# Expert lists of a mixture-of-experts block, computed at the width that each rank can hold

## The reference, cut to what matters

```python
def moe(h, router_w, router_bias, w1, w3, w2):
    ...
    _, top_idx = lax.top_k(jnp.where(in_group, sel, -jnp.inf), TOP_K)     # TOP_K = 2
    ...
    gate = jnp.sum(jax.nn.one_hot(top_idx, N_EXPERTS, dtype=f) * wts[..., None], axis=1).astype(t.dtype)
    out = jnp.zeros_like(t)
    for e in range(N_EXPERTS):
        hid = jax.nn.silu(t @ w1[e]) * (t @ w3[e])
        out = out + gate[:, e:e + 1] * (hid @ w2[e])
    return out.reshape(shp)
```

## Time and profile before

| | |
|---|---|
| median of 3 runs | 1711.62 us |
| the profiled execution's own time | 1710.11 us |
| its span | 1708.4 us |
| TensorE busy | 1548.5 us, 91% |
| VectorE busy | 1027.1 us, 60% |
| ScalarE busy | 777.4 us, 46% |
| listed steps in the trace, w3 of step 1 to w2 of step 12 | about 681 us to 929 us |
| mean granted clock of TensorE | 0.943 |

### The profile page before, as it was taken

One profiled execution on the slowest core, in us unless ns is written; L12 is line 12 of the kernel. 1 busy time (PEld: TensorE's weight loads), 2 busy tenths in 40 slices (PEclk: granted clock), 3 DMA queues, 4 the chain that ended last, 5 costly groups with the idle time before them and its releaser, 6 DMA issues.

```text
span 1708.4 us, 23313 instructions
## 1 busy us (share of the span) xinstructions
PE 1548.5 (91%) x9498; PEld 1297.2 (76%) x9498; DVE 1027.1 (60%) x1288; ACT 777.4 (46%) x937; POOL 231.2 (14%) x303
## 2 busy tenths in 40 slices
PE   4899989797668788999999989999999999999997
PEld 2678776575558667888887767779999777799996
DVE  1557446747555666777775766565444655655445
ACT  4524314551332344666665325535444556444444
POOL 0013361231241012000001350010000000000000
PEclk9899999897679888999999999989999999999999
DMA  9757620010334524898987644325544544345441
GB/s 348 276 213 271 163 50 1 7 25 5 88 97 156 205 100 173 321 325 325 324 317 263 214 148 148 112 79 196 190 175 178 196 148 148 122 163 188 178 179 72
DMA packets 152530, 294.14 MB, mean 172 GB/s; under 512 B 33538, under 2 KB 36745, under 8 KB 152424
## 3 DMA queue, kind: packets, MB, share of 16 engines
q1 hardware_dynamic: 136024, 270.50, 44.7%
q0 software_dynamic: 6464, 18.61, 3.4%
q10 hardware_dynamic: 9936, 3.54, 0.8%
HBM read 283.16 MB, written 9.47 MB: 171 GB/s over the span
## 4 chain that ended last, share of the span: by engine, by line
PE 75%; DVE 8%; issue 5%; ACT 4%; DMA 2%; DVEq 2%; SPq 1%; ACTq 1%; POOL 1%; POOLq 0%
PE psum L214 20%; PE psum L216 20%; PE psum L215 20%; PE psum L2490 3%; DMA modw<-in_mod_w_dram 1%; DVE w_low L2385 1%; PE psum L3491 1%; DMA raw<-in_w_out_dram 1%; PE psum L3515 1%; PE psum L748 1%; DVE w_low L202 1%; PE psum L765 1%; ACT w_high L179 1%; PE psum L1537 1%; DVE outer L1170 1%
## 5 line engine op out<-in xcount | busy, mean ns | idle before, releaser
L184 DVE TENSOR_TENSOR w_low<-raw,w_high 128x4096 fp32r<-128x4096 f32 (+1 forms) x60 | 265.7, 4429 | 253.4 <-ACT w_high L179 253.0
L179 ACT ACTIVATE w_high<-raw 128x4096 fp32r<-128x4096 f32 (+1 forms) x62 | 223.7, 3611 | 136.2 <-DMA raw<-in_w_up_dram 85.5
L2385 DVE TENSOR_TENSOR w_low<-raw,w_high 128x2048 fp32r<-128x2048 f32 x90 | 202.8, 2295 | 43.9 <-ACT w_high L2377 43.6
L2377 ACT ACTIVATE w_high<-raw 128x2048 fp32r<-128x2048 f32 x90 | 165.7, 1908 | 10.2 <-DMA raw<-in_moe_w_dram 10.1
L216 PE MATMUL psum<-actA_high,w_low 128*128 128x256 f32 x512 | 144.9, 283 | 0.0
L215 PE MATMUL psum<-actA_low,w_high 128*128 128x256 f32 x512 | 144.9, 283 | 0.0
L214 PE MATMUL psum<-actA_high,w_high 128*128 128x256 f32 x512 | 144.8, 283 | 0.0
L214 PE MATMUL psum<-w_high,act_high 128*128 128x512 f32 x320 | 127.8, 399 | 15.3 <-DVE act_low L1980 9.0
L215 PE MATMUL psum<-w_low,act_high 128*128 128x512 f32 x320 | 126.3, 395 | 0.0
L216 PE MATMUL psum<-w_high,act_low 128*128 128x512 f32 x320 | 126.1, 394 | 0.0
L214 PE MATMUL psum<-w_high,ff_high 128*128 128x512 f32 x256 | 100.0, 391 | 0.0
(11 more groups left out here) (570 smaller groups left out, 3482.0 us busy)
## 6 DMA issues: line engine op xcount, KB each, us to landing
raw<-in_moe_w_dram SPq DMA_DIRECT2D x90, 1024.0 KB, 6.5
raw<-in_w_in_dram SPq DMA_DIRECT2D x20, 2048.0 KB, 8.6
raw<-in_w_up_dram SPq DMA_DIRECT2D x16, 2048.0 KB, 8.0
raw<-in_w_down_dram SPq DMA_DIRECT2D x16, 2048.0 KB, 7.6
modw<-in_mod_w_dram SPq DMA_DIRECT2D x12, 2048.0 KB, 13.1
raw<-in_w_out_dram SPq DMA_DIRECT2D x6, 2048.0 KB, 8.5
raw<-in_w_gate_dram SPq DMA_DIRECT2D x4, 2048.0 KB, 7.8
raw<-in_moe_w_dram SPq DMA_DIRECT2D x3, 2048.0 KB, 8.3
```

The costliest lines, as they stand in the source:

```text
L179: act.activation(WH[n % NSLOT][:, 0:elems], RAW[n % NSLOT][:, 0:elems], ACT.Copy).then_inc(s_wh, 1)
L184: dve.tensor_tensor(WL[n % NSLOT][:, 0:elems], RAW[n % NSLOT][:, 0:elems], WH[n % NSLOT][:, 0:elems].bitcast(F32), ALU.subtract).then_inc( ...
L2377: act.activation(WH[n % NSLOT][:, ps], RAW[n % NSLOT][:, ps], ACT.Copy).then_inc(s_wh if h else X["fwh"], 1)
L2385: dve.tensor_tensor(WL[n % NSLOT][:, ps], RAW[n % NSLOT][:, ps], WH[n % NSLOT][:, ps].bitcast(F32), ALU.subtract).then_inc(s_wl if h else ...
```

## The change

Each listed step is computed on `slots_of(i)` slots, which is now rounded up to an even number (128, 102, 86, 74, 64, 56, 52, 46, 42, 40, 36, 34): the selection matrix, the moving operand of the gather, the copies into `gact`, the stationary operand of w1, w3 and w2, the partitions of silu, product and `ybuf`, and the width of the split of the hidden list. The number of instructions and their order stay as they are on every engine. There is one gather of 32 matmuls for each listed step, as before. The dense steps keep their shapes.

```diff
+    def slots_at(j):
+        return min(P, (2 * T // (j + 1) + 1) // 2 * 2)
...
     def slots_of(i):
-        return min(P, TOPK * T // (place(i) + 1))
+        return slots_at(place(i))
+
+    def rows_in(i):
+        return slots_of(i) if listed(i) else P
...
         for t in range(NT):
-            ins = pool.tensor_scalar(pickd[i % 2][:, t, :], slot1[:, :], slotk[:, t, j:j + 1], None, ALU.is_equal)
+            n = slots_of(i)
+            ins = pool.tensor_scalar(pickd[i % 2][:, t, 0:n], slot1[:, 0:n], slotk[:, t, j:j + 1], None, ALU.is_equal)
...
                     for t in range(NT):
-                        ins = pe.matmul(psum[:, gather_banks(i)[b], at:at + P], ht[:, t, P * k:P * (k + 1)],
-                                        pickd[i % 2][:, t, :], start=(t == 0), stop=(t == NT - 1))
+                        ins = pe.matmul(psum[:, gather_banks(i)[b], at:at + n], ht[:, t, P * k:P * (k + 1)],
+                                        pickd[i % 2][:, t, 0:n], start=(t == 0), stop=(t == NT - 1))
...
     def gathered(i, b):
-        return gact[i % 2][:, 2 * b:2 * b + 2, :, :].rearrange("p k w n -> p (k w n)")
+        return gact[i % 2][:, 2 * b:2 * b + 2, :, :].rearrange("p k w n -> p (k w) n")[:, :, 0:slots_of(i)]
+
+    def gather_out(i, b):
+        return psum[:, gather_banks(i)[b], :].rearrange("p (q n) -> p q n", n=P)[:, :, 0:slots_of(i)]
...
         if listed(i):
-            return gact[i % 2][:, k, 0, :], gact[i % 2][:, k, 1, :]
+            return gact[i % 2][:, k, 0, 0:slots_of(i)], gact[i % 2][:, k, 1, 0:slots_of(i)]
...
-                ins = three_pass(pe, psum[:, bank + t, :], aH, aL, wh[:, k, :], wl[:, k, :], k == 0, k == KT - 1)
+                ins = three_pass(pe, psum[0:rows_in(i), bank + t, :], aH, aL, wh[:, k, :], wl[:, k, :], k == 0,
+                                 k == KT - 1)
...
-            ins = pe.transpose(psum[:, 2 + t, P * c:P * (c + 1)], hidt[:, t, P * c:P * (c + 1)], ident[:, :])
+            m = rows_in(i)
+            ins = pe.transpose(psum[:, 2 + t, P * c:P * c + m], hidt[0:m, t, P * c:P * (c + 1)], ident[0:m, 0:m])
...
-                ts = slice(P * t, P * (t + 1))
+                ts = slice(P * t, P * t + rows_in(i))
...
-                    ins = three_pass(pe, psum[:, 4 + 2 * t + half, :], hidH[:, k, ts], hidL[:, k, ts], wh[:, k, hs],
+                    ins = three_pass(pe, psum[0:rows_in(i), 4 + 2 * t + half, :], hidH[:, k, ts], hidL[:, k, ts], wh[:, k, hs],
...
-            ins = act.activation(hidH[:, :, P * t:P * (t + 1)], bank3(2 + t), ACT.Copy)
+            m = rows_in(i)
+            ins = act.activation(hidH[:, :, P * t:P * t + m], bank3(2 + t)[:, :, 0:m], ACT.Copy)
...
-            ins = dve.tensor_tensor(hidL[:, :, ts], bank3(2 + t), hidH[:, :, ts].bitcast(F32), ALU.subtract)
+            ins = dve.tensor_tensor(hidL[:, :, ts], bank3(2 + t)[:, :, 0:rows_in(i)], hidH[:, :, ts].bitcast(F32), ALU.subtract)
```

More of the change, by code:

```diff
@@ L1851, in two_block_kernel @@
     posv = lr2.take("posv", [P, NT, E])
-    ROWS = 1 + sum(min(P, 2 * T // (j + 1)) for j in range(3, E - 1))
+    def slots_at(j):
+        return min(P, (2 * T // (j + 1) + 1) // 2 * 2)
+    ROWS = 1 + sum(slots_at(j) for j in range(3, E - 1))
     yrows = nc.dram_tensor("yrows", (ROWS, D), F32, kind="Internal").ap()
@@ L2489, in gather_tensor @@
                     for t in range(NT):
-                        ins = pe.matmul(psum[:, gather_banks(i)[b], at:at + P], ht[:, t, P * k:P * (k + 1)],
-                                        pickd[i % 2][:, t, :], start=(t == 0), stop=(t == NT - 1))
+                        ins = pe.matmul(psum[:, gather_banks(i)[b], at:at + n], ht[:, t, P * k:P * (k + 1)],
+                                        pickd[i % 2][:, t, 0:n], start=(t == 0), stop=(t == NT - 1))
             ins.then_inc(X["gat"], 1)
     def gathered(i, b):
-        return gact[i % 2][:, 2 * b:2 * b + 2, :, :].rearrange("p k w n -> p (k w n)")
+        return gact[i % 2][:, 2 * b:2 * b + 2, :, :].rearrange("p k w n -> p (k w) n")[:, :, 0:slots_of(i)]
+    def gather_out(i, b):
+        return psum[:, gather_banks(i)[b], :].rearrange("p (q n) -> p q n", n=P)[:, :, 0:slots_of(i)]
     def gather_scalar(act, i, b):
         act.wait_ge(X["gat"], since("gat", 4 * (i - 1) + b + 1))
-        act.activation(gathered(i, b), psum[:, gather_banks(i)[b], :], ACT.Copy).then_inc(X["gaA"], 1)
+        act.activation(gathered(i, b), gather_out(i, b), ACT.Copy).then_inc(X["gaA"], 1)
     def gather_vector(dve, i, b):
         dve.wait_ge(X["gat"], since("gat", 4 * (i - 1) + b + 1))
-        dve.tensor_copy(gathered(i, b), psum[:, gather_banks(i)[b], :]).then_inc(X["gaV"], 1)
+        dve.tensor_copy(gathered(i, b), gather_out(i, b)).then_inc(X["gaV"], 1)
     def rows_of(i, k, t):
         if listed(i):
-            return gact[i % 2][:, k, 0, :], gact[i % 2][:, k, 1, :]
+            return gact[i % 2][:, k, 0, 0:slots_of(i)], gact[i % 2][:, k, 1, 0:slots_of(i)]
         ts = slice(P * t, P * (t + 1))
@@ L2643, in silu_scalar @@
             act.wait_ge(M["hid"], i)
-        n = tiles_of(i)
-        act.activation(sgt[:, 0:n, :], psum[:, 0:n, :], ACT.Silu).then_inc(M["silu"], 1)
+        m, n = rows_in(i), tiles_of(i)
+        act.activation(sgt[0:m, 0:n, :], psum[0:m, 0:n, :], ACT.Silu).then_inc(M["silu"], 1)
     def hidden_scalar(act, i):
@@ L2659, in rows_scalar @@
             act.wait_ge(x_out[i % 2], x_out0[i % 2] + 16 * ((i - 1) // 2))
-        act.activation(ybuf[i % 2][:, :], psum[:, 4:6, :].rearrange("p b n -> p (b n)"), ACT.Copy
+        m = slots_of(i)
+        act.activation(ybuf[i % 2][0:m, :], psum[0:m, 4:6, :].rearrange("p b n -> p (b n)"), ACT.Copy
                        ).then_inc(X["acc"], 1)
@@ L2696, in product_vector @@
     def product_vector(dve, i):
-        n = tiles_of(i)
+        m, n = rows_in(i), tiles_of(i)
         dve.wait_ge(s_wdone, n_w3(i) + 1)
         dve.wait_ge(M["silu"], i + 1)
-        dve.tensor_tensor(hidt[:, 0:n, :], psum[:, 2:2 + n, :], sgt[:, 0:n, :], ALU.mult).then_inc(M["hid"], 1)
+        dve.tensor_tensor(hidt[0:m, 0:n, :], psum[0:m, 2:2 + n, :], sgt[0:m, 0:n, :], ALU.mult).then_inc(M["hid"], 1)
     def hidden_vector(dve, i):
```

## The result

The changed kernel takes 1724.9 us (median of 5 runs, 1723.3 to 1754.7) against 1711.3 us before: a ratio of 1.0075, interval [1.0057, 1.0093]. It is slower by some 13 us, outside my range. The same file run a second time gave 1.0103 [1.0082, 1.0124].

A forecast was written before the change was run, and what follows sets the result against it. The prediction took TensorE's own pace to bound the listed steps. Gather 0, weight matmuls 0, changes of shape +2.2, tail -1.1 and clock 0 made +1.1 us: 1712.7 us, no change, with a whole range of 1705 to 1720 us.

The forecast's parts named there:

- the term of the clock: TensorE's granted clock around the narrow gathers: taken as 0, with ends of -1.6 and +8.0 us.
- rival 2: Clock falls behind narrow gathers, in w2 of steps 5 to 12: 1.6 us each, 1720 us with 4 or 5; chance 0.25.
- my end of +8.0: Upper bound in us of the clock's cost, if 5 of the steady stretch's 10 gathers set off one half-clock stretch each.
- the changes of shape: TensorE switching between 128- and 64-column shapes from step 5 on: 24 changes at about 0.09 us, +2.2 us.
- The gather at full clock: The gather's 32 matmuls per listed step: still 3.5 us at 34 slots, so 0 gain.
- rival 3: The gather's time follows its moving columns: -21.3 us, 1691 us, faster; chance 0.05.
- The weight matmuls: The 72 matmuls of w1, w3 and w2 per listed step: pace stays 0.227 us, so 0 gain.
- rival 1: The weight matmuls' pace follows their stationary columns: -5.8 us, 1706.9 us, faster; chance 0.23.
- Tail: Shorter copies and splits before w2 of steps 11 and 12: waits shrink by 0.39 and 0.7 us, together -1.1 us.
- My test for being wrong: The forecast is wrong if the listed steps' period moves by more than 0.3 us either way.
- my sum: Gather 0, weight matmuls 0, changes of shape +2.2, tail -1.1, clock 0: +1.1 us, giving 1712.7 us.
- the transposes: Four transposes per listed step keep 128 stationary columns: 0 gain, at most -2.7 us in all.

The follow-up runs named there:

- gather_wide: The changed kernel with the selection matrix and the gather's moving operand 128 slots wide again; ratio 1.0000 [0.9970, 1.0030] to the kernel before.
- again2: The changed kernel, not edited, run once more for a profile of an execution undisturbed ahead of the change; 1732.35 us.
- gather_only: The kernel before with only the selection matrix and the gather's moving operand made narrow; ratio 1.0004 [0.9987, 1.0021].
- gather_only_pad: gather_only with two more matmuls ahead of each gather of steps 3 to 12; 1724.9 us, ratio 1.0092 [1.0064, 1.0121].
- rows66: gather_wide with rows, copies, transposes and splits at least 66 slots wide, so no 64-column shape; ratio 0.9982 [0.9965, 0.9999].
- mixed_wide: The kernel before, 128 slots everywhere, with its gather matmuls issued one by one between weight matmuls; ratio 0.9980 [0.9957, 1.0004].
- before_pad: The kernel before with two more 128-wide matmuls ahead of each gather of steps 3 to 12, nothing narrower; ratio 1.0035 [0.9999, 1.0071].
- rows66_narrow: rows66 with the gather narrow again; ratio 1.0044 [1.0013, 1.0075].
- mixed_again: Second run of rows66_narrow with gather matmuls issued one by one between weight matmuls and transposes inside w1; 1692.2 us, ratio 0.9877 [0.9845, 0.9909].

## Why the prediction was wrong

**The step that failed** is the term of the clock: "I take 0 for the forecast: the gather's stretch of 4 us with 128 columns kept 1.00 throughout." The row speaks of the wide gather, and I used it for the narrow one. The row that spoke of narrow matmuls, the fall to 0.57 behind 346 to 349 us, I had, and put down as an end. gather_wide against the changed kernel, 1.0000 against 1.0075 and 1.0103, is that term alone: some 13 to 18 us, give or take 5. In again2 the six falls in the listed steps came to 18.7 us; in the first profile those steps lost 5.9 us beside gather_wide.

My argument against rival 2 was a row read wrong. It said that stretches with such matmuls "kept 0.8 or 0.9 in most slices of the page". A slice is 43 us long, and the three slices of again2 with two falls in each read 8. An 8 leaves room for 9 to 17 us at half clock, so the row could not speak against falls of a few us.

**Its bound was too small too.** Rival 2 (0.25) named the right mechanism, and nearly the place: I had put the fall in the w2 matmuls behind the gather, and it comes inside the gather and lasts into w2. Its 1.6 us for one fall came from a stretch of 3.6 us. In again2 the clock stayed down for 6.8 us at each of six gathers: 3.1 us each, twice the price. And I let 5 of 10 gathers fall; the count was six in a row. 6 x 3.1 = 18.7 us stands against my end of +8.0.

**That the terms act together** I did not see. The +2.2 us of the changes of shape and the clock stood side by side in the sum. They are not independent: the shapes lengthen the step by 0.2 us, and with steps 0.2 us longer by other means the falls become common (gather_only against gather_only_pad). That the shapes act in the changed kernel by the step's length, and not otherwise, is argued from that pair. A fall lengthens its own step to 23.9 us, and in again2 the next gather falls again 2.1 us after its start (775.91 to 778.0, 799.81 to 801.9).

**What held.** The gather at full clock: 3.53 us, where I said 3.5 and rival 3 less. The weight matmuls: 0.23 us with 34 stationary columns, so rival 1 (0.23) is out. Changes of shape: 1.4 us measured for 20 of them, 1.8 by my rate; 27 in all at 0.07 make 1.9, where I had 2.2. Tail: the waits shrank by 0.32 and 0.63 us, where I had 0.39 and 0.7. The copies that ScalarE and VectorE were spared bought nothing in the steady stretch. My test for being wrong, a period that moves by more than 0.3 us, was met: a step with a fall took 3.3 us longer than the 20.57 before.

**A small term that did not hold.** I took 0 for the transposes because they keep 128 stationary columns. They went from 0.44 to 0.26 us for four. The steps didn't get shorter by it: in rows66 the gather starts 0.12 us sooner behind the first transpose, but a step's w3 and w1 took 11.11 us on average against 11.06 before and its w2 5.59 against 5.53. Why the weight matmuls are that little slower stays open.

Without the clock my sum gave 1712.7 us, +0.06%; the kernel in which the clock doesn't fall, gather_wide, measured 1.0000.

## What to carry to other kernels

Don't count on fewer moving columns to shorten short matmuls that load 128 stationary columns each: the gather here kept 0.11 us each from 128 moving columns down to 34, and the engine only did less in the same time. The transposes, which got narrower in rows and in moving columns, did speed up, so read the pace for each kind from the trace. A block of such matmuls can cost the granted clock, without any idle time to warn of it; take the bound for it from a stretch with operands that narrow, count every block, and don't add it beside a term that moves the blocks in time. If narrow operands are to pay, try spreading the short matmuls between the long ones: here, with both narrow and nothing under 66 stationary columns in the weight matmuls, that turned +0.8% into -1.2%, while spreading alone changed nothing that is clear of noise (mixed_wide).

## What the runs showed of the hardware that I had not expected

- The granted clock fell to 0.50 with TensorE busy all of the time, in the middle of blocks of 32 matmuls with 34 to 52 moving columns, 2.2 to 2.3 us after their start (again2), and between 710 and 900 us in no profile of a kernel whose gather moves 128 (the kernel before, gather_wide, rows66, before_pad, mixed_wide). The engine's busy time by the trace was whole in both cases, so it does not warn of this.
- The same kernel took 1706 to 1709 us or 1719 to 1726 us (rows66_narrow); its three profiles have no, one or three falls of 6.8 us. The Trainium skill ("TensorE: Matmul & The Clock Gate", Part 1: The HAM clock gate) says that what watches the engine runs free and isn't aligned to the kernel's start. That would make the loss a matter of where a block lands, and agrees with the two groups and with the effect of 0.22 us more in a step; no run here set the place of a block by itself.
- Between two matmuls of 512 columns a gather matmul costs 0.06 us where it moves 40 columns beside 66 stationary ones (mixed_again), and 0.11 with 128 and 128 (mixed_wide).
- A gather matmul with 128 stationary columns keeps 0.11 us down to 34 moving columns (gather_only), but a transpose, with 128 stationary columns too, takes 0.06 us with 74 rows and 74 moving columns where it took 0.11 with 128 of each (again2 against before).
